# Conditioning blocks of layer 0's gate/up stage: one per pair, or two in every second pair

## The reference, cut to what matters

```python
mod = silu(c) @ w_ada[i] + b_ada[i]              # shift1, scale1, gate1, shift2, scale2, gate2
h = x * (1 + scale1) + shift1
mix = mixer(h)                                   # input projection, attention and convolution, w_out
x = layernorm(ALPHA * x + gate1 * mix)
h = x * (1 + scale2) + shift2
f = (silu(h @ w_gate) * (h @ w_up)) @ w_down     # D_FF = 2816 = 22 tiles of 128
x = layernorm(ALPHA * x + gate2 * f)
```

## Time and profile before

| | |
|---|---|
| median of three runs | 1505.82 us (1505.09 to 1506.27) |
| the profiled execution | 1505.4 us, of which the span from the first to the last instruction is 1503.5 us |
| TensorE busy | 1431.0 us, 95% of the span |
| VectorE, ScalarE, GpSimd busy | 69%, 44%, 6% |
| DMA | 197 MB, mean 131 GB/s |
| mean granted clock of TensorE | 0.978 of full speed |

### The profile page before, as it was taken

How to read it: one execution, slowest core, us unless ns; L and a number is a source line. 1 busy time by engine, 2 the same in 40 slices (tenths; PEclk the granted TensorE clock), 3 DMA queues, 4 the chain that set the end, 5 groups by cost and what they waited for, 6 DMA issues and landing times.

```text
span 1503.5 us, 26963 instructions
## 1 busy us (share of the span) xinstructions
PE 1431.0 (95%) x11064; PEld 1293.7 (86%) x11064; DVE 1036.2 (69%) x1754; ACT 666.4 (44%) x1161; POOL 94.8 (6%) x112
## 2 busy tenths in 40 slices
PE   7999988999999999999989999889899999999996
PEld 5887766878999999999979977659799999999995
DVE  2799884458877777822448989855788888892333
ACT  4425566236444444611245245662555544461132
POOL 1000000112000000001020000002200000000100
PEclk9999999998999999999989999999899999999998
DMA  9778345451444444422214553441113223223221
GB/s 368 232 170 216 114 197 199 154 197 57 169 169 169 168 169 169 151 88 87 82 45 148 75 160 115 196 143 62 65 57 111 87 88 110 85 67 100 80 64 63
DMA packets 61545, 197.19 MB, mean 131 GB/s; under 512 B 22768, under 2 KB 23152, under 8 KB 51184
## 3 DMA queue, kind: packets, MB, share of 16 engines
q1 hardware_dynamic: 61424, 195.48, 39.3%
HBM read 187.27 MB, written 8.18 MB: 130 GB/s over the span
## 4 chain that ended last, share of the span: by engine, by line
PE 77%; DVE 10%; ACT 5%; issue 2%; DMA 2%; ACTq 0%; SPq 0%; DVEq 0%
PE ps L1594 33%; PE ps L1620 29%; PE ps L1726 2%; PE ps L1636 2%; DVE sb_y L1155 2%; PE ps L2041 2%; PE ps L1759 1%; ACT sb_E L759 1%; PE ps L1645 1%; DVE sb_w_lo L1058 1%; DMA sb_w_raw<-w_mix 1%; PE ps L1870 1%; PE ps L1698 1%; PE ps L1834 1%; PE ps L1793 1%
## 5 line engine op out<-in xcount | busy, mean ns | idle before, releaser
L1594 PE MATMUL ps<-sb_h,sb_w_hi 128*128 128x288 f32 x1632 | 314.0, 302 | 1.4 <-DVE sb_uS L1373 1.4
L1594 PEld LDWEIGHTS ps<-sb_h,sb_w_hi 128*128 128x128 f32 x1632 | 243.7, 188 | 36.7 <-issue 33.7
L1620 PE MATMUL ps<-sb_tt,sb_w_hi 128*128 128x288 f32 x1280 | 269.3, 296 | 2.5 <-DVE sb_up L1513 1.6
L640 ACT ACTIVATE sb_w_hi<-sb_w_raw 128x1024 fp32r<-128x1024 f32 x112 | 118.3, 1057 | 292.0 <-PE ps L1594 268.6
L1058 DVE TENSOR_TENSOR sb_w_lo<-sb_w_raw,sb_w_hi 128x1024 fp32r<-128x1024 f32 x112 | 136.4, 1221 | 156.4 <-ACT sb_w_hi L640 156.1
L1620 PEld LDWEIGHTS ps<-sb_tt,sb_w_hi 128*128 128x128 f32 x1280 | 210.1, 188 | 3.2 <-DVE sb_up L1513 2.0
L1620 PE MATMUL ps<-sb_h,sb_w_hi 128*128 128x288 f32 x960 | 206.3, 297 | 0.1
L1620 PE MATMUL ps<-sb_tt,sb_w_lo 128*128 128x288 f32 x640 | 189.4, 296 | 0.0
L1594 PE MATMUL ps<-sb_h,sb_w_lo 128*128 128x288 f32 x816 | 174.1, 294 | 0.0
L1620 PEld LDWEIGHTS ps<-sb_h,sb_w_hi 128*128 128x128 f32 x960 | 158.6, 188 | 17.1 <-DVE sb_w_lo L1065 15.9
L1155 DVE SCALAR_TENSOR_TENSOR sb_y<-sb_uP,sb_vec,sb_y 128x512 f32<-128x512 f32 x240 | 164.9, 744 | 0.5
(11 more groups left out here) (248 smaller groups left out, 2139.8 us busy)
## 6 DMA issues: line engine op xcount, KB each, us to landing
sb_w_raw<-w_mix SPq DMA_DIRECT2D x104, 512.0 KB, 3.9
sb_ring<-w_ada SPq DMA_DIRECT2D x42, 1024.0 KB, 6.0
sb_w_two<-w_mix SPq DMA_DIRECT2D x40, 512.0 KB, 4.5
sb_w_raw<-w_dn SPq DMA_DIRECT2D x32, 512.0 KB, 3.6
sb_ring<-vc_d SPq DMA_DIRECT2D x12, 1024.0 KB, 7.6
sb_ring<-kc_d SPq DMA_DIRECT2D x8, 1024.0 KB, 7.6
sb_w_raw<-w_dn SPq DMA_DIRECT2D x16, 384.0 KB, 3.1
sb_big<-w_ada SPq DMA_DIRECT2D x5, 1024.0 KB, 11.1
```

The costliest lines, as they stand in the source:

```text
L640: nc.scalar.activation(w_hi[:, slot(n):slot(n) + 2, :], w_raw[:, u % 2, :].rearrange("p (h n) -> p h n", h=2), ACT.Copy)\
L1594: ins = nc.tensor.matmul(z[:, i], a[:, at, w], b(k0 + k)[:, i * H:(i + 1) * H], start=first and k == 0 and t == 0, stop=last and k == nk - ...
L1620: ins = nc.tensor.matmul(ps[:, FAST_BANK[j], 0:H], a[:, slot(n), w], moving(j, k, part), start=j < P2 and k == 0 and t == 0, stop=k == KT ...
```

## The change

The hook of the gate/up stage multiplied quad 24+i in every pair i: for pair 0 behind its products, for pair 1 ahead of its last k step, and from pair 2 on ahead of P3. Now it does nothing in even pairs and multiplies quads 24+i-1 and 24+i in odd pairs, at the same place. The turns of quads 24 to 31 and 32 to 39 move from pairs 8 and 16 to pairs 9 and 17, ahead of the two quads there. Nothing else is changed: neither the order of the loads in SP's queue, nor the copies and biases on ScalarE and VectorE.

```diff
                 def gate_up(i):
                     def hook(k):
-                        if l == 0 and k == 7:
-                            n = GU_QUAD0 + i
-                            if i in (8, 16):
+                        if l == 0 and k == 7 and i % 2:
+                            n = GU_QUAD0 + i - 1
+                            if i in (9, 17):
                                 ada_turn(n // KT - 1)
-                            ada_quad(n)
+                            for q in range(n, n + 2):
+                                ada_quad(q)
                     return hook
 
-                if l == 0:
-                    gate_up(0)(7)
                 for i in range(1, PLAIN):
```

## The result

| | before | after |
|---|---|---|
| median | 1505.21 us (7 runs, 1503.82 to 1508.31) | 1500.45 us (7 runs, 1499.28 to 1501.70) |
| ratio | | 0.9975, 95% interval 0.9964 to 0.9985 |
| profiled execution, span | 1505.4 us, 1503.5 us | 1500.42 us, 1498.5 us |
| P4 of pair 2 to the first product of the down projection | 241.07 us | 237.92 us |
| the rest of the span | 1262.4 us | 1260.6 us |

The change makes the kernel faster, by a quarter of a per cent. So the prediction was wrong in its numbers. Its main mechanism, the saved change of form, was right, as the stage shows; the late up tile, its other term, did not come about in the usual pair.

What follows compares the result with a forecast made beforehand. TensorE was taken to bound the pairs, its chain 77% of the span. Ten merges save 3.0 us and the late up tile costs 0.2: span 1500.7 us, median 1503.0 us, range 1501.8 to 1506.2 us.

Steps and rivals of the forecast that it cites:

- the saved change of form: Layer 0's gate/up stage, pairs 2 to 21: ten merges each save 0.30 us of entering and leaving the narrow form, 3.0 us.
- the late up tile: Odd pairs 3 to 21: up tile issued later, `add_first` 0.3 us late, at times 1.4; 0.2 us lost in all.
- A quad costs 1.17 us and the second of two 0.87: TensorE, layer 0's gate/up stage: a lone quad costs 1.17 us, a second one right behind it 0.87 us.
- no saving: Rival: each quad pays its 1.17 us wherever it stands, time 1505.8 us; chance 0.15, shared with half the saving.
- Pairs 0 and 1 give nothing: First merge, where the chain runs over ScalarE and VectorE: quads already hidden, gain at most 0.3 us.
- The cadence of 11.19 us in even pairs: Layer 0's gate/up stage: even pairs without quads take 11.19 us, odd ones 13.23 us, and VectorE keeps up.
- 1.3 us of cover: Between line 1513's end on VectorE (405.83) and P4's first weights (407.13): a late `add_first` costs TensorE nothing within it.
- Quad 46 in time: Stage's end: quad 46 lands at T0 + 7.2, needed at T0 + 7.8, so no wait, 0.6 us in hand.
- The sum: Whole span: 1503.5 - 3.0 + 0.2 = 1500.7 us, profiled execution 1502.6, median 1503.0 us.
- the term for the scatter: Whole kernel: 0.8 us allowed for scatter in setting the range's low end, 1501.8 us.
- The bound of 0.2%: Whole kernel: a change is told from none from about 3.0 us, 1502.8 us down; faster 0.43, within 0.47, slower 0.10.
- the up tile ends last: Rival, slower: up tile lands at T0 + 8.5 to 9.6, P4 waits 0 to 1.0 us, up to 1512.8 us; chance 0.15.

Runs made afterwards that it cites:

- e3: Changed kernel with the odd pair's two quads apart, one ahead of P4 and one ahead of P3: stage 241.20 us, ratio 1.0006 to the kernel before.
- e6: Changed kernel with quads 24 and 25 alone in pairs 0 and 1 as before: stage 237.73 us, ratio 0.9981 to the kernel before.
- e5: Changed kernel with both quads behind P3 of the odd pair instead of ahead of it: stage 246.93 us, ratio 1.0039 to the kernel before.
- e7: Changed kernel with quads 26 to 43 multiplied in the even pair behind, between P6 and P7: stage 286.62 us, ratio 1.0302 to the kernel before.

## Why the prediction was wrong, and what of it held

- *A quad costs 1.17 us and the second of two 0.87.* Held, and a little better: 24.38 instead of 24.72 us in two pairs is 0.34 us a merge, so the second quad costs 0.83. e3 shows that it is the change of form that is saved and that "no saving" is out. Ten merges: 3.4 us instead of 3.0.
- *Pairs 0 and 1 give nothing.* Held, shown by e6.
- *The cadence of 11.19 us in even pairs.* Held: two pairs of matmuls take 22.53 us, 2 x 11.19 and 0.15 us of the way in and out, and TensorE has no wait among them.
- *The late up tile costs 0.2 us.* Held as a sum, not as a mechanism. `add_first` was to be 0.3 us late in odd pairs, and in the usual pair it was not late at all: T0 + 7.33 was predicted for the need and 7.31 measured, but the landing came at T0 + 7.2 instead of 7.6. The issue went faster by 0.1 and the load by 0.3 us. The one load of 7.2 us cost 0.18 us, and the two other profiles show 0. The waits in e5 and e7 fit the 1.3 us of cover within 0.2 us. The Trainium skill's figure for a load (DMA: Bandwidth & Descriptors, Anatomy of one DMA) gives T0 + 1.13 + 5.6 = T0 + 6.7 as an estimate (the prediction says 6.8); it was below the landing, and the rows' 7.6 above it.
- *Quad 46 in time.* Held: issued at 614.89 and landed 4.7 us later, needed at 621.45, and TensorE has no wait for it.
- *The sum.* -2.8 us was predicted for the stage, and -3.15, -3.37 and -3.38 measured in three profiles of the changed kernel (237.92, 237.73 and 237.72 against 241.10). This part of the prediction was low by 0.35 to 0.6 us, 0.04 us in each merge and the load that was not late.
- **The step that failed is the term for the scatter**, with a small part from the price of a merge. The low end of the range was "the sum, the first merge and 0.8 us of scatter" (1501.9 by its own terms; it says 1501.8), from three runs that lay within 1.2 us. The profiled execution was forecast at 1502.6 us and took 1500.42: of the 2.2 us between, 0.35 are the stage, and 1.8 are the rest of the span, 1260.6 instead of 1262.4 us, which the prediction took as fixed. 0.8 us is far too little for that. Three profiles of the kernel before share a stage of 241.1 us, and its runs beside the experiments lay from 1496.8 to 1508.6 us; the rest of the span went from 1255.5 to 1265.1 us over thirteen profiles. 3.4 us of 1505 would be a ratio of 0.9977. The three comparisons of the changed kernel gave 0.9975, 0.9983 and 0.9984, all with that value in their interval. So of the 4.8 us between the two medians 3.1 to 3.4 are the change in the stage, and the rest is scatter as far as the runs can tell. The mean of the three ratios is 0.9981, 2.9 us; a further effect of about 1 us, one way or the other, would not be seen. Why one execution has more stretches of low clock than another stays open.
- *The bound of 0.2%.* The forecast sat on it (2.8 us is 0.19%), and 0.35 to 0.6 us more in the stage were enough to cross it: 3.4 us is 0.23%. The other 0.02% of the measured 0.25% are luck.
- *The rival "the up tile ends last"* did not happen. It had only the waits in it, up to 1.0 us each. e5 and e7 show that longer waits, of 2 to 3 us, can cost more by the clock that falls behind them: 1.5 us behind one of e5's two and nothing behind the other, and 2.1 us in the mean of e7's nine. For waits as short as the rival's no run shows such a cost.

## What to carry to other kernels

Where two kinds of matmul alternate, count the changes between them: here the way into a narrow form and out again was together 0.3 us of a 1.2 us insert, and putting the inserts side by side saved it without any other change. A double insert needs its buffers twice as long, so look at the load queue next: whether the freed buffer's load, and all that stands behind it, still lands in time, and whether both buffers now come free at once. To measure 3 us in 1500, compare the length of the stage between two fixed instructions (within 0.2 us here) and not the total (12 us from lowest to highest).

## What the runs showed of the hardware that was not expected

- A wait of TensorE of 2.1 us in a stage at full clock was followed, from 406.2 to 409.5 us, by matmuls 0.24 us apart instead of 0.133 (e5). The granted clock fell from 1.00 to 0.50, the lower of its levels (1.2 GHz), and it cost 1.5 us on top. With nine waits of 3.3 us in the mean (e7) the clock of the stage was 0.93 and the cost on top 19 us. But it does not follow each wait: behind 2.54 us in e5 and behind one of 3.25 us in e7 the clock stayed at 1.00. A wait of 0.6 us in e5 showed little of it: the two pairs with it took 25.25 us, 0.87 more than 24.38. The Trainium skill (TensorE: Matmul & The Clock Gate, What's actually happening) gives two states of this gate, 1.2 GHz idle and 2.4 GHz busy; the traces agree on the two levels, 0.50 from 406.2 to 409.5 and 1.00 ahead of the wait.
- Sixteen narrow products with a passed semaphore wait in their middle ran as close together (1.85 us with the way out, some 0.13 us) as the sixteen of the earlier trace rows without one (1.74 us).
- A 512 KB tile right behind a 1 MB quad landed 5.5 to 6.0 us after its issue in nearly all pairs of the three profiles of the changed kernel; one of thirty took 7.2 us. In e5 two took 7.7 and 8.2 us, and the first of them cost 3.9 us.
